# Latent gates in the last scan stage: sigmoid on ScalarE, or exponential on ScalarE and one-plus and reciprocal on VectorE

## The chip, the cores and the metric

The kernel runs on one core of a Trainium2 chip. The metric is the device time of one execution in microseconds (us), the median of several runs.

## The reference

Two layers of a hybrid sequence model, for 1024 prompt positions and 8 sample sequences of 16 new positions each, 1152 positions in all, everything in f32. Per layer:

```python
proj = h @ P['w_in'][l]
pr, zA, cq, ckv, kr, zB, sq, sk, sv, zC, gates = _split(proj, IN_SIZES)
yA, S1, shift1 = rwkv7_branch(pr, shift0, S0, P, l)       # a recurrence over time, 8 heads of 64
yB, ckv1, kr1 = mla_branch(cq, ckv, kr, ckv0, kr0, q_pos, k_pos, P, l)
yC, k1, v1 = sb_branch(sq, sk, sv, k0, v0, q_pos, k_pos)
merged = (gA * ((yA * jax.nn.silu(zA)) @ P['w_br_rwkv'][l])
          + gB * ((yB * jax.nn.silu(zB)) @ P['w_br_mla'][l])
          + gC * ((yC * jax.nn.silu(zC)) @ P['w_br_sb'][l]))
```

The change concerns `silu(zB)`, the gate of the latent attention branch: silu(z) = z times sigmoid(z) = z / (1 + exp(-z)). Half of its 512 columns (two pieces of 128 by 1152) are made in the stage that the change touches.

## The kernel before

A layer is a row of stages; between two stages all engines meet at a barrier. The recurrence (`rwkv`) takes two heads at a time, so there are four rounds `h` = 0 to 3. Each round has a stage `rwkv_solve` and then a stage `rwkv_fused(..., h, nx)`, which runs the scan of round `h` and, beside it, prepares round `nx` = `h + 1`. In the last round there is nothing to prepare (`nx` is None, `prep` is False). TensorE then fills its free time with the latent gates instead: `GATE_FILL`, six units of eight matmuls (one unit is z for 384 positions of one piece, `hT` times `w_piece`, L1052). This last stage occurs once in each layer, so twice in the kernel.

The scan goes over 16 chunks of 64 positions, one after another, and each needs the state of the one before. In chunk `n`:

- TensorE multiplies the state (L1101) and does one fill matmul ("mid").
- VectorE adds this to `z_solved` (L1282, semaphore `u_added`).
- TensorE makes the state's update from it (L1104) and the outputs (L1107), and does one fill matmul ("end").
- VectorE makes the new state (L1288, semaphore `s_scaled`), and TensorE's next chunk waits for it. A decayed copy of the state comes from GpSimd (L1015).

A program's fill matmul is two instructions in the trace, since f32 goes through TensorE in two passes. `gate_chunk` says in which chunk a unit's results are taken: units 0 and 1 ahead of chunk 0, units 2 to 5 in chunks 2, 6, 10 and 14. For a unit, ScalarE waits for the unit's last matmul and writes the sigmoid of the PSUM bank to `temp` (L1133). VectorE waits for that and multiplies it by the bank (`latent_gates`, L1273, semaphore `g_made`). VectorE does this in its own program order: behind the state of chunk 2, 6, 10 or 14 and ahead of the `z_solved` addition of the next chunk. Units from 2 on reuse one of two banks, so a unit's first matmul waits for the `g_made` of the unit two before it.

Beside this the engines normalise finished groups of outputs. VectorE forms sums (L1225 to L1229) at chunks 3, 7, 12 and behind the scan. ScalarE makes the reciprocal root as Ln and Exp (L1203, L1204) at `n` = 4, 8, 13 and 16. VectorE multiplies (L1234) at 5, 10, 14 and 16, TensorE transposes (L1067) ahead of chunks 11 and 15 and at the end, and VectorE applies the gate of this branch (L1239, L1240). ScalarE also copies two chunks' outputs behind each odd chunk (L1197, L1198).

ScalarE can only compute functions of the table set that it has loaded. The program loads a set by `preload_act_table_set`; where an activation needs a function that the active set lacks, the compiler puts a load ahead of it. `own(...)` makes an engine wait for its own instruction before it starts the next.

Of the kernel before, what the change touches and what calls it, by code (L numbers as in the profile page):

```python
# [8 lines left out]
ALU = mybir.AluOpType  # L9
ACT = mybir.ActivationFunctionType  # L10
# [15 lines left out]
NTG = T // TG  # L26
# [877 lines left out]
def rwkv_fused(nc, S, A, O, l, ps, con, hT, yg, zg, ahead, R, h, nx):  # L904
# [3 lines left out]
    V, ACTE = nc.vector, nc.scalar  # L908
# [4 lines left out]
             "state_out", "u_ready", "u_added", "y_ready", "y_copied", "s_ready", "s_scaled",  # L913
             "stat_in", "stat_out", "y_normed", "y_turned", "y_gated", "y_stored", "z_gated", "sd_made", "g_sigmoid", "g_made", "g_stored", "ahead_loaded", "ends_stored", "vec", "act_own")
    with S.stage(*names) as (block, sb, (w0_loaded, w1_loaded, par_done, fill_ready, free0, free1, summed, exps_done,
                                         z_sigmoid, shifted, squared, maxed, rooted, prod_done, r_done, k_stored, rv_stored,
                                         state_out, u_ready, u_added, y_ready, y_copied, s_ready, s_scaled,
                                         stat_in, stat_out, y_normed, y_turned, y_gated, y_stored, z_gated, sd_made, g_sigmoid, g_made, g_stored, ahead_loaded, ends_stored, vec, act_own)):
        free = (free0, free1)
# [32 lines left out]
        def cols(g):  # L952
            return slice(TG * g, TG * g + TG)
# [169 lines left out]
        def _(act):  # L1123
            own = InOrder(act, act_own)

            def evacuate(n):
# [5 lines left out]
                if kind == "g":  # L1132
                    ACTE.activation(t[g // NTG][:, c], src, ACT.Sigmoid).then_inc(g_sigmoid, 1)  # L1133
                    return
# [27 lines left out]
            if scan:  # L1162
                ACTE.activation(t[2][:, :], R.zs[h % 2][:, :], ACT.Sigmoid).then_inc(z_sigmoid, 1)
            for n in range(-1, NCK + 1):
                for q in range(len(fills)):
                    if chunk_of(q) == n:
                        evacuate(q)
                if n == 1:
                    ACTE.preload_act_table_set("natural_log_exp_and_others")
# [37 lines left out]
        def _(dve):  # L1207
# [60 lines left out]
            def latent_gates(n):  # L1268
                for q in range(len(fills)):
                    if not prep and chunk_of(q) == n:  # L1270
                        dve.wait_ge(g_sigmoid, q + 1)
                        c = cols(q % NTG)
                        V.tensor_tensor(t[q // NTG][:, c], t[q // NTG][:, c], ps[:, q % 2, 0:TG], ALU.mult).then_inc(g_made, 1)  # L1273

# [1562 lines left out]
```

## Time and profile before

| what | us |
|---|---|
| median of 3 runs | 4704.79 (4702.94 to 4711.39) |
| the profiled execution, its own time | 4707.36 |
| its span, first to last instruction | 4705.5 |
| last scan stage of layer 0, in the span | 712.5 to 793.6 |
| last scan stage of layer 1, in the span | 3057.4 to 3138.7 |

The profiled execution took 2.6 us more than the median of the runs. Times inside a stage are given from the span's start. A row of the timeline has the start, how long it took, the engine, the line, the operation and its tiles, how many instructions were merged in it, and in brackets the idle time of the engine ahead of it and what ended that.

### The profile page before, as it was taken

The page shows a single profiled execution, that of the slowest core. Times are in us where ns is not written, and L with a number is a line of the kernel's source. Part 1 is how long each engine was busy: PE and PEld are TensorE (multiplying, and loading weights), DVE is VectorE, ACT ScalarE, POOL GpSimd, SP SyncE. Part 2 cuts the span into 40 slices and gives each one's busy share as a digit, 9 for nine tenths or more (in the row PEclk, how much of TensorE's full clock was granted, in tenths as well). Part 3 has the DMA queues.
Part 4 walks back from the last instruction along what each step waited for, and adds up shares of the span by engine and source line. Part 5 has one row for each costly group of instructions (what it writes and reads, how often), then busy time and mean ns, then how long its engine had stood idle before and what let it go on. Part 6 is the DMA issues. An engine that isn't in the chain of part 4 may idle for free. (4 is left out here: it accounts for less than half of the span.)

```text
span 4705.5 us, 74875 instructions
## 1 busy us (share of the span) xinstructions
PE 4334.4 (92%) x29488; PEld 3017.3 (64%) x29488; DVE 2280.0 (48%) x4684; ACT 1643.2 (35%) x3886; POOL 814.2 (17%) x980
## 2 busy tenths in 40 slices
PE   7999998989989989999979999989888999899999
PEld 3666665667666667777436666655666566677774
DVE  2556664345524453534425665633455244535344
ACT  4333433445523442211043334333555234421220
POOL 0011010000010015544300110000000100245443
PEclk9999998999999999999989999999999999999999
DMA  5110012010021112222241210120100211123222
GB/s 195 23 35 13 28 25 87 14 36 14 12 87 56 53 65 92 95 102 76 85 192 23 35 15 26 25 88 17 31 16 11 87 58 57 70 88 111 89 72 84
DMA packets 150655, 280.77 MB, mean 60 GB/s; under 512 B 51546, under 2 KB 77402, under 8 KB 145059
## 3 DMA queue, kind: packets, MB, share of 16 engines
q1 hardware_dynamic: 150306, 275.99, 18.3%
q8 instruction: 236, 3.87, 0.4%
q14 instruction: 113, 0.92, 0.1%
HBM read 230.96 MB, written 42.62 MB: 58 GB/s over the span
## 5 line engine op out<-in xcount | busy, mean ns | idle before, releaser
L1054 PE MATMUL banks<-hT,w_piece 128*128 128x384 f32 x1536 | 545.2, 496 | 4.4 <-ACT raw L1159 4.1
L1054 PEld LDWEIGHTS banks<-hT,w_piece 128*128 128x128 f32 x1536 | 279.4, 193 | 171.6 <-issue 11.8
L2233 PE MATMUL banks<-hT,w_piece 128*128 128x384 f32 x1056 | 354.1, 489 | 1.5 <-ACT sb_gate_raw L2343 1.5
L2233 PEld LDWEIGHTS banks<-hT,w_piece 128*128 128x128 f32 x1056 | 196.1, 190 | 141.4 <-issue 16.6
L1999 DVE SCALAR_TENSOR_TENSOR keysT<-banks,gains,rstd 64x128 f32<-64x128 f32 (+1 forms) x272 | 112.1, 412 | 252.9 <-ACT rstd L1913 250.4
L2689 DVE TENSOR_TENSOR gate_quarters<-gate_kept,banks 128x288 f32<-128x288 f32 x144 | 65.4, 454 | 298.4 <-PE banks L2552 293.4
L2640 ACT ACTIVATE gate_kept<-banks 128x288 f32<-128x288 f32 x144 | 59.0, 410 | 431.9 <-PE banks L2552 431.9
L2689 DVE TENSOR_TENSOR branch_quarters<-branch_kept,banks 128x288 f32<-128x288 f32 x144 | 65.4, 454 | 265.0 <-PE banks L2552 264.7
L2405 DVE TENSOR_TENSOR_SCAN left<-pass,zero 128x384 f32<-128x384 f32 (+7 forms) x144 | 190.5, 1323 | 5.0
L2402 DVE TENSOR_TENSOR pass<-pass,constants 128x128 f32<-128x128 f32 x128 | 40.8, 319 | 312.8 <-ACT take L2354 310.2
L1015 POOL TENSOR_TENSOR state_decayed<-state,decay_of_chunk 128x128 f32<-128x128 f32 x120 | 85.9, 716 | 547.4 <-DVE state L1288 547.4
L1831 PE MATMUL banks<-keysT,queriesT 96*128 96x512 f32 (+3 forms) x384 | 155.3, 514 | 8.7 <-DVE queriesT L1999 8.7
L2552 PE MATMUL banks<-hT,w_gate_ahead 128*128 128x288 f32 x576 | 153.6, 418 | 7.7 <-PEq L132 7.4
L2552 PE MATMUL banks<-y_branch,w_branch 128*128 128x288 f32 x576 | 155.4, 406 | 0.0
L2552 PE MATMUL banks<-hT,w_gate 128*128 128x288 f32 x576 | 147.5, 406 | 0.0
L2552 PEld LDWEIGHTS banks<-hT,w_gate_ahead 128*128 128x128 f32 x576 | 112.7, 196 | 41.4 <-issue 9.3
L1929 ACT ACTIVATE exponentials<-banks,maximum 128x384 f32<-128x384 f32 (+4 forms) x144 | 104.1, 723 | 91.8 <-DVE maximum L2012 90.1
L1940 ACT ACTIVATE exponentialsT<-banks 128x512 f32<-128x512 f32 (+3 forms) x208 | 94.9, 488 | 115.8 <-PE banks L1843 114.9
L2213 POOL TENSOR_TENSOR sb_outT<-sb_outT,sb_gate 128x128 f32<-128x128 f32 x72 | 34.9, 484 | 579.3 <-ACT sb_outT L2375 578.2
L2230 PE MATMUL banks<-w_piece,hT 128*128 128x128 f32 x1152 | 132.7, 276 | 0.0
L2644 ACT ACTIVATE gate_quarters<-gate_quarters 128x288 f32<-128x288 f32 x144 | 63.5, 441 | 195.6 <-DVE gate_quarters L2689 195.1
L2230 PEld LDWEIGHTS banks<-w_piece,hT 128*128 128x128 f32 x1152 | 130.2, 192 | 1.0
(425 smaller groups left out, 9801.8 us busy)
## 6 DMA issues: line engine op xcount, KB each, us to landing
w_piece<-in_w_cols SPq DMA_DIRECT2D x66, 512.0 KB, 4.4
w_ada<-in_w_ada SPq DMA_DIRECT2D x24, 1024.0 KB, 9.6
w_gate_ahead<-in_w_cols SPq DMA_DIRECT2D x48, 512.0 KB, 4.3
w_branch<-in_w_br SPq DMA_DIRECT2D x96, 256.0 KB, 2.9
w_gate<-in_w_cols SPq DMA_DIRECT2D x48, 512.0 KB, 4.3
y_branch<-y_gated SPq DMA_DIRECT2D x12, 1152.0 KB, 8.0
sb_cached_keysT<-in_sbkT SPq DMA_DIRECT2D x8, 1024.0 KB, 7.6
sb_cached_values<-in_sbv SPq DMA_DIRECT2D x8, 1024.0 KB, 5.1
```

The lines of the kernel that those rows point to most:

```text
L1015: G.tensor_tensor(SD[:, :], ST[:, :], R.pend[h % 2][:, n + 1:n + 2].broadcast_to([P, P]), ALU.mult).then_inc(sd_made, 1)
L1054: last = mm(dst, w[0 if kind in ("k", "v") else 1][:, k, :], hT[:, k, c], start=(k == 0), stop=(k == KD - 1))
L1831: last = mm(ps[:, b0 + a // 512, 0:e - a], Q[hh][:, P * i:P * i + P], K[hh][:, a:e], start=True, stop=True)
L1929: do(E[u % 3][:, 0:width(u)], sbank(u)[:, 0:width(u)], ACT.Exp, bias=mx[:, u:u + 1], scale=scale, accum_out=rsum[:, u:u + 1]).then_inc(exp ...
L1940: do(ET[:, s % 4, units[u][3], 0:cnt, :].rearrange("p q n -> p (q n)"), ps[:, ring_bank(("t", u, g)), 0:P * cnt], Copy).then_inc(ring_free, 1)
L1999: ins = V.scalar_tensor_tensor(to[hh][0:64, c], ps[hc, bank[n], at], par[hc, gain:gain + 1], rs[x % 2][hc, at], ALU.mult, ALU.mult)
L2230: last = mm(ps[:, bank[n], P * q:P * q + P], hT[:, k, P * i:P * i + P], w_of[wn][:, k, :], start=(k == 0), stop=(k == KD - 1))
L2233: last = mm(ps[:, bank[n], 0:TG], w_of[wn][:, k, :], hT[:, k, TG * g:TG * g + TG], start=(k == 0), stop=(k == KD - 1))
L2405: own(V.tensor_tensor_scan(mine[:, 0:n][:, ::-1], G[k][:, 0:n][:, ::-1], zero[:, 0:1].broadcast_to([P, n]), 1.0, ALU.mult, ALU.add))
L2552: ins = mm(ps[:, bank, 0:TQ], w[:, k, :], b[:, k, :], start=(first and k == 0), stop=(k == half - 1), skip_group_check=True)
L2644: do(gq[:, q, :], gq[:, q, :], ACT.Tanh, scale=0.5).then_inc(tanh_done, 1)
L2689: own(V.tensor_tensor(dst, src, ps[:, bank, 0:TQ], ALU.add), added)
```

## The change

In the last stage, ScalarE writes exp(-z) instead of sigmoid(z), and VectorE adds one and takes the reciprocal before it multiplies by z. The set with both the logarithm and the exponential is loaded right behind the one sigmoid that stays (that of the recurrence's own gate), ahead of all six units, instead of at `n` = 1. The other `rwkv_fused` stages keep their instructions.

```diff
@@ scalar, evacuate
                 act.wait_ge(fill_ready, n + 1)
                 if kind == "g":
-                    ACTE.activation(t[g // NTG][:, c], src, ACT.Sigmoid).then_inc(g_sigmoid, 1)
+                    ACTE.activation(t[g // NTG][:, c], src, ACT.Exp, scale=-1.0).then_inc(g_exp, 1)
                     return
@@ scalar
             if scan:
                 ACTE.activation(t[2][:, :], R.zs[h % 2][:, :], ACT.Sigmoid).then_inc(z_sigmoid, 1)
+            if not prep:
+                ACTE.preload_act_table_set("natural_log_exp_and_others")
             for n in range(-1, NCK + 1):
...
-                if n == 1:
+                if prep and n == 1:
                     ACTE.preload_act_table_set("natural_log_exp_and_others")
@@ vector, latent_gates
-                        dve.wait_ge(g_sigmoid, q + 1)
+                        dve.wait_ge(g_exp, q + 1)
                         c = cols(q % NTG)
+                        own(V.tensor_scalar(t[q // NTG][:, c], t[q // NTG][:, c], 1.0, None, ALU.add))
+                        own(V.reciprocal(t[q // NTG][:, c], t[q // NTG][:, c]))
                         V.tensor_tensor(t[q // NTG][:, c], t[q // NTG][:, c], ps[:, q % 2, 0:TG], ALU.mult).then_inc(g_made, 1)
```

ScalarE's instructions from the start of layer 1's last stage to chunk 4, before (`temp_25` holds the gates, `silu_z_16` the recurrence's gate):

```order
L1161 ACT_TABLE_LOAD
L1163 ACTIVATE temp_25<-silu_z_16 128x1152
L1133 ACTIVATE temp_25<-banks 128x384 x2
L1169 ACT_TABLE_LOAD
L1197 ACTIVATE z_solved<-banks 64x128
L1198 ACTIVATE z_solved<-banks 64x128
L1133 ACT_TABLE_LOAD
L1133 ACTIVATE temp_25<-banks 128x384
L1197 ACTIVATE z_solved<-banks 64x128
L1198 ACTIVATE z_solved<-banks 64x128
L1203 ACT_TABLE_LOAD
L1203 ACTIVATE statistics<-statistics,constants 128x2
```

And now, at the same place, up to the Exp of the first statistics:

```order
L1161 ACT_TABLE_LOAD
L1163 ACTIVATE temp_25<-silu_z_16 128x1152
L1165 ACT_TABLE_LOAD
L1133 ACTIVATE temp_25<-banks 128x384 x2
L1199 ACTIVATE z_solved<-banks 64x128
L1200 ACTIVATE z_solved<-banks 64x128
L1133 ACTIVATE temp_25<-banks 128x384
L1199 ACTIVATE z_solved<-banks 64x128
L1200 ACTIVATE z_solved<-banks 64x128
L1205 ACTIVATE statistics<-statistics,constants 128x2
L1206 ACTIVATE statistics<-statistics 128x2
```

The load of L1169 moved ahead of the first two units, and no other load is left in the stage: ScalarE has 3298 instructions where it had 3322 (runs of equal ones counted once), 12 fewer in each of the two stages.

VectorE's instructions around the first two units and chunk 0 of the same stage, before:

```order
L1266 TENSOR_TENSOR sample_states<-banks,decay_of_chunk_16 128x512
L1273 TENSOR_TENSOR temp_25<-temp_25,banks 128x384 x2
L1282 TENSOR_TENSOR bk_and_vu_rows<-z_solved,banks 64x128
L1288 SCALAR_TENSOR_TENSOR state<-banks,decay_of_chunk_16,state_decayed 64x64 x2
L1282 TENSOR_TENSOR bk_and_vu_rows<-z_solved,banks 64x128
```

And now:

```order
L1268 TENSOR_TENSOR sample_states<-banks,decay_of_chunk_16 128x512
L1275 TENSOR_SCALAR temp_25<-temp_25 128x384
L1276 RECIPROCAL temp_25<-temp_25 128x384
L1277 TENSOR_TENSOR temp_25<-temp_25,banks 128x384
L1275 TENSOR_SCALAR temp_25<-temp_25 128x384
L1276 RECIPROCAL temp_25<-temp_25 128x384
L1277 TENSOR_TENSOR temp_25<-temp_25,banks 128x384
L1286 TENSOR_TENSOR bk_and_vu_rows<-z_solved,banks 64x128
L1292 SCALAR_TENSOR_TENSOR state<-banks,decay_of_chunk_16,state_decayed 64x64 x2
```

Four instructions came in ahead of the first addition to `z_solved`.

VectorE's instructions at chunk 14, the last unit, before:

```order
L1288 SCALAR_TENSOR_TENSOR state<-banks,decay_of_chunk_16,state_decayed 64x64 x2
L1273 TENSOR_TENSOR temp_25<-temp_25,banks 128x384
L1234 TENSOR_TENSOR z_solved<-z_solved,statistics 128x384
L1282 TENSOR_TENSOR bk_and_vu_rows<-z_solved,banks 64x128
L1288 SCALAR_TENSOR_TENSOR state<-banks,decay_of_chunk_16,state_decayed 64x64 x2
```

And now:

```order
L1292 SCALAR_TENSOR_TENSOR state<-banks,decay_of_chunk_16,state_decayed 64x64 x2
L1275 TENSOR_SCALAR temp_25<-temp_25 128x384
L1276 RECIPROCAL temp_25<-temp_25 128x384
L1277 TENSOR_TENSOR temp_25<-temp_25,banks 128x384
L1236 TENSOR_TENSOR z_solved<-z_solved,statistics 128x384
L1286 TENSOR_TENSOR bk_and_vu_rows<-z_solved,banks 64x128
```

The two new instructions stand between the state of chunk 14 and both things that TensorE needs next, the normalised outputs and the addition of chunk 15.

## Rows read from the trace of the kernel before

**Rows 1.** The page: busy time of each engine.

```profile
PE 4334.4 (92%) x29488; PEld 3017.3 (64%) x29488; DVE 2280.0 (48%) x4684; ACT 1643.2 (35%) x3886; POOL 814.2 (17%) x980
```

**Rows 2.** Both last scan stages: busy PE, PEld, DVE, ACT, POOL; clock; DMA, GB/s.

```profile
712.50:793.60 81.10, 60.17 (x261) 37.07 (x261) 41.73 (x103) 28.42 (x45) 8.71 (x16) 0.88 0.10 34
3057.40:3138.70 81.30, 58.53 (x261) 36.04 (x262) 41.72 (x103) 28.42 (x45) 8.71 (x16) 0.90 0.10 34
```

**Rows 3.** Timeline of VectorE, layer 0, first two units to chunk 3.

```profile
731.34 1.02 DVE L1273 TENSOR_TENSOR temp<-temp,banks 128x384 f32<-128x384 f32 x2
733.77 0.29 DVE L1282 TENSOR_TENSOR bk_and_vu_rows<-z_solved,banks 64x128 f32<-64x128 f32 x1 [1.41 <-PE banks L1101]
...
736.03 0.28 DVE L1282 TENSOR_TENSOR bk_and_vu_rows<-z_solved,banks 64x128 f32<-64x128 f32 x1 [0.73 <-PE banks L1101]
...
738.27 0.29 DVE L1282 TENSOR_TENSOR bk_and_vu_rows<-z_solved,banks 64x128 f32<-64x128 f32 x1 [0.75 <-PE banks L1101]
...
740.83 0.55 DVE L1273 TENSOR_TENSOR temp<-temp,banks 128x384 f32<-128x384 f32 x1 [1.05 <-ACT temp L1133]
741.30 0.27 DVE L1282 TENSOR_TENSOR bk_and_vu_rows<-z_solved,banks 64x128 f32<-64x128 f32 x1
```

**Rows 4.** Timeline of TensorE at the same places.

```profile
731.95 1.56 PE L1052 MATMUL banks<-hT,w_piece 128*128 128x384 f32 x4 [1.45 <-DVE temp L1273]
...
739.34 0.86 PE L1052 MATMUL banks<-hT,w_piece 128*128 128x384 f32 x2
...
741.63 0.49 PE L1104 MATMUL banks<-bk_and_vu_rows 128*128 128x128 f32 x2 [0.56 <-DVE bk_and_vu_rows L1282]
```

**Rows 5.** ScalarE, layer 0: timeline of chunk 2; the gates' activations of the whole stage.

```profile
737.85 1.28 ACT L1133 ACT_TABLE_LOAD   x1
740.24 0.49 ACT L1133 ACTIVATE temp<-banks 128x384 f32<-128x384 f32 x1 [1.10 <-PE banks L1052]
...
L1133 ACT ACTIVATE temp<-banks 128x384 f32<-128x384 f32 x6 | 2.9, 490 | 15.5 <-PE banks L1052 15.5
```

**Rows 6.** VectorE's reciprocal and scalar operation of this shape, both in other stages, whole kernel.

```profile
L1572 DVE RECIPROCAL rope_rstd<-rope_rstd 128x384 f32<-128x384 f32 x12 | 30.6, 2553 | 19.7 <-ACT rope_rstd L1533 19.6
L2019 DVE TENSOR_SCALAR exponentials<-exponentials,row_sums 128x384 f32<-128x384 f32 x32 | 13.4, 420 | 1.2
```

**Rows 7.** Timeline of layer 1 at chunk 14: TensorE, ScalarE, VectorE.

```profile
3121.14 0.86 PE L1052 MATMUL banks<-hT,w_piece 128*128 128x384 f32 x2
...
3122.79 1.28 ACT L1133 ACT_TABLE_LOAD   x1
3124.08 0.49 ACT L1133 ACTIVATE temp<-banks 128x384 f32<-128x384 f32 x1
...
3125.75 0.90 PE L1067 MATMUL banks<-constants,z_solved 128*128 128x128 f32 x3 [3.75 <-DVE z_solved L1234]
```

**Rows 8.** The same of layer 0: TensorE's last fill, and ScalarE's activation.

```profile
777.71 0.86 PE L1052 MATMUL banks<-hT,w_piece 128*128 128x384 f32 x2
...
779.05 0.49 ACT L1133 ACTIVATE temp<-banks 128x384 f32<-128x384 f32 x1
```

**Rows 9.** Timeline of layer 0 behind the scan: ScalarE, VectorE.

```profile
787.05 1.28 ACT L1204 ACT_TABLE_LOAD   x1
...
787.39 0.62 DVE L1240 SCALAR_TENSOR_TENSOR k_shifted<-k_shifted,parameters,silu_z 128x384 f32<-128x384 f32 x1
788.65 0.42 DVE L1234 TENSOR_TENSOR z_solved<-z_solved,statistics 128x256 f32<-128x256 f32 x1 [0.64 <-ACT statistics L1204]
```

**Rows 10.** Granted clock around the idle time of TensorE, both layers.

```profile
772.00:776.00 4.00, 2.86 (x11) 2.16 (x12) 1.70 (x6) 1.90 (x4) 0.40 (x1) 0.75 0.00 0
3126.00:3130.00 4.00, 2.62 (x11) 2.14 (x10) 1.09 (x4) 0.87 (x3) 0.00 (x0) 0.50 0.37 147
```

**Rows 11.** TensorE in layer 0 at the lower clock: two chunks' L1104.

```profile
773.14 0.49 PE L1104 MATMUL banks<-bk_and_vu_rows 128*128 128x128 f32 x2 [1.65 <-DVE bk_and_vu_rows L1282]
...
776.84 0.63 PE L1104 MATMUL banks<-bk_and_vu_rows 128*128 128x128 f32 x2
```

More of the change, by code:

```diff
@@ L913, in rwkv_fused @@
              "state_out", "u_ready", "u_added", "y_ready", "y_copied", "s_ready", "s_scaled",
-             "stat_in", "stat_out", "y_normed", "y_turned", "y_gated", "y_stored", "z_gated", "sd_made", "g_sigmoid", "g_made", "g_stored", "ahead_loaded", "ends_stored", "vec", "act_own")
+             "stat_in", "stat_out", "y_normed", "y_turned", "y_gated", "y_stored", "z_gated", "sd_made", "g_exp", "g_made", "g_stored", "ahead_loaded", "ends_stored", "vec", "act_own")
     with S.stage(*names) as (block, sb, (w0_loaded, w1_loaded, par_done, fill_ready, free0, free1, summed, exps_done,
@@ L917, in rwkv_fused @@
                                          state_out, u_ready, u_added, y_ready, y_copied, s_ready, s_scaled,
-                                         stat_in, stat_out, y_normed, y_turned, y_gated, y_stored, z_gated, sd_made, g_sigmoid, g_made, g_stored, ahead_loaded, ends_stored, vec, act_own)):
+                                         stat_in, stat_out, y_normed, y_turned, y_gated, y_stored, z_gated, sd_made, g_exp, g_made, g_stored, ahead_loaded, ends_stored, vec, act_own)):
         free = (free0, free1)
```

## The prediction

> **What bounds the kernel now.** I read the page first: TensorE is busy for 92% of the span, VectorE for 48%, ScalarE for 35% [rows 1]. That is an average over the whole kernel, and the change touches two stages of some 81 us each, 162 of 4705.5 us. So I read those two by themselves. In them TensorE is busy for 60.2 and 58.5 us of 81, VectorE for 41.7 and ScalarE for 28.4 [rows 2]. None of the three is full. A stage like this is bound by a chain from engine to engine, and the timeline shows which links it has.
>
> An ordinary chunk of the scan takes 736.03 to 738.27, 2.24 us from one addition L1282 to the next, and VectorE waits 0.73 to 0.75 us ahead of each for TensorE [rows 3]. That is the slack that VectorE has in a chunk without other work. At chunk 2 it is different. VectorE waits 1.05 us for ScalarE, then multiplies the unit, and the addition of chunk 3 starts only behind that, at 741.30. TensorE waits 0.56 us for this addition [rows 3, 4]. So where a unit is taken, VectorE's own program order puts the gate on the path of the recurrence, with no slack left. This happens at chunks 2, 6, 10 and 14. The first two units are taken ahead of chunk 0: TensorE waits 1.45 us for the first of them (it needs the bank), and then VectorE waits 1.41 us for TensorE [rows 3, 4].
>
> Next I ask what ScalarE is late for. At chunk 2 its table load starts at 737.85 and is over at 739.13. Then it still waits 1.10 us for TensorE, whose last fill matmul ends at 739.34 + 0.86 = 740.20, and the activation starts at 740.24 [rows 4, 5]. So the load is hidden there. Over the stage of layer 0, ScalarE's idle time ahead of these activations is 15.5 us, all of it ended by TensorE's fill [rows 5]; chunks 6 and 10 have the same 1.1 us in the timeline. Only chunk 14 differs. In layer 1 the last fill ends at 3121.14 + 0.86 = 3122.00, but a row of three loads ends at 3124.08 [rows 7].
>
> **What the change removes.** Twelve table loads in each stage, 24 x 1.283 = 30.8 us of ScalarE's time. What of it lies on the path is little:
> - Chunks 2, 6 and 10, both layers: nothing, since TensorE's fill ends last.
> - Chunk 14, layer 1: the activation could start at 3122.00 + 0.04 = 3122.04 in place of 3124.08, a gain of 2.04 [rows 7].
> - Chunk 14, layer 0: at 777.71 + 0.86 + 0.04 = 778.61 in place of 779.05, a gain of 0.44 [rows 8].
> - Behind the scan: VectorE waits 0.64 us for the statistics, which stand behind one load. VectorE starts 788.65 - 787.05 - 1.28 = 0.32 us behind the load's end, so without the load it could start at 787.37. It is itself busy until 787.39 + 0.62 = 788.01, so it starts at about 788.04 in place of 788.65 [rows 9]. A gain of 0.61, in both layers, 1.22.
>
> Together 2.04 + 0.44 + 1.22 = 3.7 us. The load that moves ahead of the units costs nothing: of the 15.5 us of idle time, some 12 lie ahead of these two.
>
> The Trainium skill ("ScalarE: Activation LUTs", section "What ACT_TABLE_LOAD costs") gives 2.66 us for a switch of sets, of which 1.38 us are a drain. Here an activation starts within 0.02 us of a load's end (3122.79 + 1.28 against 3124.08), so by the rows a switch costs 1.28 us; by the page the 24 would hold 64 us of ScalarE.
>
> **What the change adds.** Per unit, VectorE gets an addition and a reciprocal of 128 x 384 in SBUF. The trace has both shapes elsewhere. The reciprocal took 2.553 us in each of 12, and the operation with a scalar 0.420 us [rows 6]. With some 0.03 us between instructions that wait for each other, a unit gets 0.45 + 2.58 = 3.03 us more. The scalar operation of the row takes its factor from a column and this one a constant, which may differ by a tenth of a microsecond either way; the reciprocal has the same shape, type and place, so I hold it for certain within 0.1.
>
> - Units 2 to 5: ScalarE's result comes when it came before (exponential and sigmoid are both one activation). VectorE then starts its addition to `z_solved` 3.03 us later, and TensorE, which had waited already, waits 3.03 us more. 4 x 3.03 = 12.1 us per layer. Nothing can be caught up later, since the chunks run one after another at 2.24 us, and TensorE's own work in one fills nearly all of this.
> - Units 0 and 1, ahead of chunk 0: VectorE needs 6.06 us more, and 1.41 us of that is the wait that it has now ahead of the first addition [rows 3]. TensorE is released by the first unit, after 3.03, and is then ready well ahead of VectorE. 6.06 - 1.41 = 4.65 us per layer.
>
> That makes 16.8 us per layer, 33.5 in all, less 3.7 is 29.8 us. What waits behind VectorE in those 3 us is the whole scan: TensorE's update, ScalarE's copies, GpSimd's decayed state. The statistics for chunks 11 and 15 stand behind the gates on VectorE too and move along with them, at no extra price.
>
> **The clock.** TensorE's idle stretches grow from 0.56 to about 3.6 us at chunks 2 and 6, from 1.45 to 4.5 ahead of chunk 0, and by as much at chunk 10, where TensorE waits for the normalised outputs that stand behind the unit on VectorE. In the trace an idle stretch of 3.75 us [rows 7] is followed by the lower level, 1.2 in place of 2.4 GHz (0.50 in the rows behind it), and after some shorter ones in layer 0 the clock fell too, for part of a stretch (0.75) [rows 10]. A chunk in layer 0 at the lower level took 773.14 to 776.84, 3.70 us, so 1.46 more than the ordinary 2.24 [rows 11]. So each of the four longer stalls ahead of chunk 14 probably brings a low stretch of about this kind. Its price is between nothing (it falls within the stall, or beside VectorE's sums, where TensorE waits anyway) and about 2.9 us (two chunks). I take 0.9 each, near the lower end: the stalls at chunks 2 and 6 are followed by a chunk in which VectorE's sums make TensorE wait already (as the 1.65 us ahead of 773.14 [rows 11]), and the stretch begins within the stall. 8 x 0.9 = 7.2 us. The stall at chunk 14 is followed by the low level already now.
>
> Sum: 29.8 + 7.2 = 37.0 us. Against the profiled execution that is 4707.4 + 37 = 4744; against the median of the runs, which is 2.6 us lower, 4704.8 + 37 = 4742 us.
>
> **The rivals.** A measurement of this kernel can tell about 0.2%, 9.4 us, from no change.
> - The clock stays at its upper level. For it: the 1.45 us ahead of chunk 0 left no slow chunk behind them [rows 3, 4]. Against it: 3.75 us did [rows 7, 10]. It gives 29.8, so 4735 us, within the range.
> - The clock stays low through the scans. All 16 chunks of both layers at 3.70 instead of 2.24 would be 32 x 1.46 = 47 us more, 4782 us. Against it: in layer 0 the level was back within one chunk or two.
> - VectorE's work is hidden, and ScalarE decides. If what ends VectorE's waits of 1.05 us were the loads, and the new operations fitted in its idle time (39.4 of 81 us per stage; both stages together get 36 us), the kernel would be faster: the 1.28 us of a load at each of eight units and twice at the end, 12.8 us, so 4692 us. It decides only if VectorE could run the gates in another order than ahead of the next addition, which an engine with one instruction stream can't. The Trainium skill's rule to group activations by their table set ("ScalarE: Activation LUTs", section "Rules for kernel authors") speaks for this way, and the row at chunk 2 against it, where TensorE's fill ends last.
> - The reciprocal is as fast as other operations of its width, 0.56 us: a unit gets 1.04 us more, the first two 0.67 together, so 4.8 us per layer, 9.7 less 3.7 is 6 us, no change that can be told, 4711 us. The twelve equal rows speak against it.
>
> **How the numbers follow.** I give the forecast with some price of the clock, 25 to 50 us slower, 0.83; the upper rival (over 53 us) 0.07; something that hides most of the added work, within 9.4 us, 0.04; faster 0.02; and 0.04 for a slowdown of 10 to 25 us through slack that I overlooked. Slower by over 0.2% is then 0.94, the same 0.04, faster 0.02. For the range I take 29.8 less 5 us for slack in the first units and the small terms, and 29.8 plus the full 8 x 2.9 = 23 us of clock: 4730 to 4758 us. The likeliest value lies below the middle, because I hold the full price for rare.
>
> **What would show it.** In the changed kernel's trace: no load of tables in the two stages but two at the start; a reciprocal of 2.55 us x12 at the line of the gates; an addition of 0.4 us; TensorE waits of about 3.6 us for the addition to `z_solved` at chunks 2 and 6; 4.5 us ahead of chunk 0; both stages about 98 to 102 us long in place of 81; granted clock below the 0.88 and 0.90 of now; nothing else in the kernel changed by more than 1 us. I would be wrong in the main thing if the stages grew by less than 10 us each, which would mean slack between VectorE and TensorE that the rows don't show, and wrong in the clock if single chunks of 3.7 us were absent or were most of the scan.

## The result, and the profile after

The changed kernel took 4734.54 us (median of 5 runs, 4722.78 to 4738.90) against 4706.47 us (5 runs, 4702.94 to 4712.83) on the same chip: ratio 1.0054, interval 1.0039 to 1.0069. By the ratio it is 25 us slower, by the medians 28. A second set of runs gave 1.0046 (1.0030 to 1.0062), 22 us. The forecast was 37. The profiled execution took 4722.78 us, the shortest of its five; its span is 4720.9 us, 15.4 above that of before (4705.5).

The page, busy time of each engine (for [rows 1]), and below it the windows of the two last scan stages (for [rows 2]: length, busy PE, PEld, DVE, ACT, POOL, granted clock, DMA share, GB/s):

```profile
PE 4331.1 (92%) x29488; PEld 3016.0 (64%) x29488; DVE 2312.9 (49%) x4708; ACT 1617.3 (34%) x3862; POOL 814.0 (17%) x980
```

```profile
705.90:806.20 100.30, 68.07 (x261) 42.92 (x262) 59.21 (x115) 13.03 (x33) 8.73 (x16) 0.80 0.08 28
3065.70:3165.00 99.30, 67.12 (x262) 42.49 (x262) 59.19 (x115) 13.02 (x33) 8.73 (x16) 0.79 0.08 28
```

The stages grew by 19.2 and 18.0 us to 100.3 and 99.3 (98 to 102 was forecast), 37.2 together, and VectorE's busy time in each by 17.5. ScalarE has twelve instructions fewer in each. The groups of VectorE at the gates, layer 0 (six units):

```profile
L1276 DVE RECIPROCAL temp<-temp 128x384 f32<-128x384 f32 x6 | 15.3, 2553 | 0.2
L1277 DVE TENSOR_TENSOR temp<-temp,banks 128x384 f32<-128x384 f32 x6 | 3.3, 554 | 0.2
L1275 DVE TENSOR_SCALAR temp<-temp 128x384 f32<-128x384 f32 x6 | 2.2, 359 | 4.2 <-ACT temp L1133 4.2
```

And the timelines of VectorE, TensorE and ScalarE at the places of [rows 3 to 5]: first two units, chunk 2, and the later stalls.

```profile
724.65 0.36 DVE L1275 TENSOR_SCALAR temp<-temp 128x384 f32<-128x384 f32 x1
...
731.67 0.29 DVE L1286 TENSOR_TENSOR bk_and_vu_rows<-z_solved,banks 64x128 f32<-64x128 f32 x1
...
740.16 0.36 DVE L1275 TENSOR_SCALAR temp<-temp 128x384 f32<-128x384 f32 x1 [1.05 <-ACT temp L1133]
740.55 2.55 DVE L1276 RECIPROCAL temp<-temp 128x384 f32<-128x384 f32 x1
743.14 0.55 DVE L1277 TENSOR_TENSOR temp<-temp,banks 128x384 f32<-128x384 f32 x1
743.61 0.27 DVE L1286 TENSOR_TENSOR bk_and_vu_rows<-z_solved,banks 64x128 f32<-64x128 f32 x1
```

```profile
728.24 2.93 PE L1052 MATMUL banks<-hT,w_piece 128*128 128x384 f32 x4 [4.43 <-DVE temp L1277]
...
743.94 0.49 PE L1104 MATMUL banks<-bk_and_vu_rows 128*128 128x128 f32 x2 [3.54 <-DVE bk_and_vu_rows L1286]
744.66 1.53 PE L1052 MATMUL banks<-hT,w_piece 128*128 128x384 f32 x2
...
774.85 1.12 PE L1067 MATMUL banks<-constants,z_solved 128*128 128x128 f32 x4 [4.69 <-DVE z_solved L1236]
793.88 0.90 PE L1067 MATMUL banks<-constants,z_solved 128*128 128x128 f32 x3 [4.69 <-DVE z_solved L1236]
```

```profile
708.33 1.28 ACT L1165 ACT_TABLE_LOAD   x1
...
739.56 0.49 ACT L1133 ACTIVATE temp<-banks 128x384 f32<-128x384 f32 x1 [2.40 <-PE banks L1052]
```

Chunk 2 reads as before, with one thing put in. VectorE waits the same 1.05 us for ScalarE; ScalarE, with no load any more, waits 2.40 us for TensorE where it had a load of 1.28 and a wait of 1.10. So the load was hidden, to within 0.02 us. Then come 0.36 + 2.55 us of new work, and TensorE waits 3.54 us where it waited 0.56. Behind that stall the same two fill matmuls take 1.53 us where they took 0.86 [rows 4]: the clock fell to its lower level (granted 0.65 from 746 to 749 us, and 1.00 in the 3 us behind that).

Since the chunks run in a fixed chain, the time from one addition to `z_solved` to the next gives the whole stage by chunk. These are differences of the starts in VectorE's timeline, in us (chunk 1 is the time from chunk 0's addition to chunk 1's; L0, L1 are the layers):

| chunk | 1 | 2 | 3 | 4 | 5 | 6 | 7 | 8 | 9 | 10 | 11 | 12 | 13 | 14 | 15 | sum |
|---|---|---|---|---|---|---|---|---|---|---|---|---|---|---|---|---|
| before, L0 | 2.26 | 2.24 | 3.03 | 3.02 | 2.26 | 2.25 | 3.03 | 4.09 | 2.26 | 2.24 | 4.63 | 3.61 | 4.11 | 3.07 | 6.26 | 48.36 |
| after, L0 | 3.68 | 2.25 | 6.01 | 3.12 | 3.33 | 2.25 | 6.01 | 4.39 | 3.28 | 2.24 | 8.28 | 4.39 | 4.11 | 2.24 | 8.06 | 63.64 |
| before, L1 | 2.26 | 2.25 | 3.03 | 3.02 | 2.26 | 2.25 | 3.03 | 4.09 | 2.26 | 2.24 | 4.63 | 3.61 | 4.11 | 2.25 | 7.11 | 48.40 |
| after, L1 | 3.09 | 2.25 | 6.01 | 3.69 | 2.40 | 2.24 | 6.02 | 4.40 | 3.13 | 2.25 | 8.63 | 4.03 | 4.10 | 2.25 | 8.06 | 62.55 |

Chunks 3 and 7 are 2.98 us longer: the new work and nothing else. Chunks 1, 5 and 9, which stand behind the stalls, are 1.42, 1.07 and 1.02 longer in layer 0, and 0.83, 0.14 and 0.87 in layer 1: the clock. Where the low stretch lies differently, chunk 4 has a part of it (3.69 for 3.02 in layer 1).

So the stages grew by what was forecast, to the microsecond, and yet the kernel is 22 to 28 us slower and not 37. The difference lies in a stage that the change doesn't touch. Windows of the latent pairs stage (no line of it differs), both layers, before and after:

```profile
945.30:1330.70 385.40, 335.51 (x2521) 254.97 (x2521) 203.84 (x571) 206.58 (x518) 26.49 (x103) 0.94 0.07 20
3290.50:3675.60 385.10, 335.31 (x2521) 254.73 (x2521) 203.75 (x570) 206.43 (x518) 26.36 (x103) 0.94 0.07 20
```

```profile
957.60:1335.00 377.40, 327.12 (x2521) 249.10 (x2521) 203.83 (x570) 206.92 (x518) 26.57 (x103) 0.97 0.07 21
3314.90:3692.30 377.40, 327.70 (x2521) 250.32 (x2521) 203.74 (x570) 206.91 (x518) 26.48 (x103) 0.97 0.07 21
```

The instructions are the same in number, VectorE and ScalarE are busy for as long as before, but TensorE is granted 0.97 in place of 0.94, and is busy for 8 us less. It starts with the first matmuls, before and after in layer 0:

```profile
945.31 3.75 PE L1780 MATMUL banks<-latentT,weights_ahead 128*128 128x256 f32 x8 [3.22 <-PEq L132]
```

```profile
957.63 1.97 PE L1784 MATMUL banks<-latentT,weights_ahead 128*128 128x256 f32 x8 [3.21 <-PEq L132]
```

TensorE idles for 3.2 us as it enters this stage. Before, the first eight matmuls then run at the lower level (3.75 us), after at the upper (1.97). In layer 1 the first eight are slow in both kernels, but in the changed one the next sixteen are at full speed already. Before and after:

```profile
3290.45 3.75 PE L1780 MATMUL banks<-latentT,weights_ahead 128*128 128x256 f32 x8 [3.40 <-PEq L132]
3293.99 3.11 PE L1799 MATMUL banks<-weights_ahead,latentT 128*128 128x128 f32 x16
```

```profile
3314.86 3.65 PE L1784 MATMUL banks<-latentT,weights_ahead 128*128 128x256 f32 x8 [3.21 <-PEq L132]
3318.33 1.97 PE L1803 MATMUL banks<-weights_ahead,latentT 128*128 128x128 f32 x16
```

The granted clock of the first 6 us of the stage in layer 0, before and after:

```profile
945.30:951.30 6.00, 5.99 (x20) 5.28 (x21) 0.56 (x2) 2.02 (x3) 0.53 (x2) 0.50 0.78 165
```

```profile
957.60:963.60 6.00, 5.97 (x36) 5.51 (x37) 0.56 (x2) 3.03 (x5) 0.55 (x2) 1.00 0.79 171
```

The difference goes on behind the entry. In pieces of 64 us, the second is at 0.97 before and 1.00 after:

```profile
1009.30:1073.30 64.00, 59.83 (x467) 46.07 (x467) 36.05 (x96) 38.31 (x91) 4.70 (x21) 0.97 0.02 6
```

```profile
1021.60:1085.60 64.00, 59.22 (x481) 46.45 (x480) 37.01 (x98) 39.32 (x95) 5.17 (x22) 1.00 0.02 7
```

The sum over the profiled executions: +37.2 in the last scan stages, -15.7 in the two latent pairs stages, 21.5 together. The spans differ by 15.4. The remaining -6.1 is a sum of moves in both directions in stages that the change doesn't touch: -7.5 in the first preparing scan stage of layer 0 (87.1 us before, 79.6 after), +4.3 in a later one of that layer (105.3 and 109.6), +3.3 in the first of layer 1 (80.4 and 83.7), and smaller ones that sum to -6.2.

### The profile page after: what moved, and what is told of

It is laid out like the page before. It is cut to its first block and busy times, and to the rows that moved or that the text cites. A ratio compares the mean times of both kernels' runs of the same rounds, so it can differ in the third digit from the quotient of the medians.

```text
span 4720.9 us, 74875 instructions
## 1 busy us (share of the span) xinstructions
PE 4331.1 (92%) x29488; PEld 3016.0 (64%) x29488; DVE 2312.9 (49%) x4708; ACT 1617.3 (34%) x3862; POOL 814.0 (17%) x980
```

## The experiments

In all, "stages" are the two last scan stages, "pairs" the two latent pairs stages; what they gained or lost is against 81.1 + 81.3 and 385.4 + 385.1 of before. Lengths of stages are read to 0.1 us, so a sum of four holds to about 0.2.

**Each kernel once more.** The first question was whether 385 and 377 belong to the kernels or to single executions.

> The kernel before once more, for a second profile of it. If lengths outside the change move by coincidence of the clock, some of its stages differ from those of its first profile by 2 to 8 us, the latent pairs stages (385.4 and 385.2 us before) among them, with a sum within 8 us. If a kernel's stages repeat, all of them are within 1 us, and the 8 us at latent pairs belong to the change. The two last scan stages are 81 us in any case.

> The changed kernel once more, for a second profile. Two questions are open after the first: its two last scan stages grew by 19.3 and 18.3 us, 37.6 together, but its span only by 15.4, since the stages outside the change were shorter by 22 us in that one execution. If those 22 us are a coincidence of TensorE's clock in this one execution, the two stages are again 99 to 101 us long here, the other stages differ from the kernel before by less than 12 us in sum, and the span is 4726 to 4738. If the change itself shortens what follows (the latent pairs stage was 8 us shorter in both layers), that stage is again shorter by 8 us twice.

The kernel before: stages 81.1 and 81.1, pairs 385.4 and 385.1, as in its first profile (its runs: ratio 0.9988, 0.9976 to 1.0001). The changed kernel: stages 99.2 and 99.3, pairs 378.9 and 377.0. One window of each, layer 0:

```profile
943.40:1328.80 385.40, 335.46 (x2521) 254.92 (x2521) 203.79 (x571) 206.86 (x518) 26.55 (x103) 0.94 0.07 20
```

```profile
956.20:1335.10 378.90, 328.72 (x2520) 250.31 (x2521) 203.78 (x570) 206.54 (x518) 26.55 (x103) 0.96 0.07 21
```

So in the four pairs stages of each kernel's two profiles, the two kernels don't overlap. The first preparing stage took 86.3 and 82.3 us in these profiles, and 80 to 87 in others.

**The exponential without VectorE's part.** The changed kernel; it leaves out the addition of one and the reciprocal, so that the gates hold z times exp(-z). It shows what the loads were worth.

```
-                        own(V.tensor_scalar(t[q // NTG][:, c], t[q // NTG][:, c], 1.0, None, ALU.add))
-                        own(V.reciprocal(t[q // NTG][:, c], t[q // NTG][:, c]))
```

> The changed kernel without VectorE's two new operations: ScalarE writes exp(-z), the table loads are gone, and VectorE multiplies as before; left out is adding one and the reciprocal, so half of the latent gates are z times exp(-z). Theory one, that VectorE's new work is the price and the loads were mostly hidden: against before 3.7 us less, more exactly 0.5 + 0.6 in layer 0 and 2.0 + 0.6 in layer 1, and up to 2 more where TensorE's clock stays up; the stages take 78 to 80.5 us each. Theory two, that the loads were on the path: 12.8 us less at least, up to 30.8 (all 24 loads of 1.283 us), the stages 66 to 75 us each.

Ratio 0.9952 (0.9937 to 0.9966). The windows of both stages:

```profile
705.00:784.60 79.60, 59.75 (x262) 36.63 (x262) 41.73 (x103) 13.02 (x33) 8.73 (x16) 0.89 0.10 35
3046.50:3126.10 79.60, 59.75 (x261) 36.62 (x261) 41.71 (x103) 13.06 (x33) 8.75 (x16) 0.89 0.10 35
```

They are 1.5 and 1.7 us shorter: 24 loads, 30.8 us of ScalarE, were worth 3.2 us. Chunks 1 to 13 are the same as before within 0.02 us each; only the steps to chunks 14 and 15 changed (5.43 for 6.26 in layer 0; in layer 1 5.42 for 7.11, but 3.03 for 2.25 ahead of it, where the lower clock now fell). The sum of the two steps is 0.9 us less in each layer. The kernel as a whole gained 23 us, seven times as much, and 15.5 of that is pairs at 377.5 us in both layers. That the loads were "worth 0.5%" would be the wrong reading of the time alone: in the stages they were worth 3.2 us.

**VectorE's part without the exponential.** The kernel before, with an addition of one and a reciprocal on a spare tile ahead of each multiplication; sigmoid and loads stay.

```
+            spare = None if prep else sb("spare_gate", [P, TG])
...
+                        own(V.tensor_scalar(spare[:, :], t[q // NTG][:, c], 1.0, None, ALU.add))
+                        own(V.reciprocal(spare[:, :], spare[:, :]))
```

> The kernel before, with its sigmoid and all its table loads, and an addition and a reciprocal of 128 x 384 on VectorE ahead of each multiplication, into a spare tile that nothing reads. Theory one: each of units 2 to 5 costs 2.97 us, the first two 4.6 together, so 16.5 us per layer and some 4 more for TensorE's lower clock: stages of 101 to 103 us, 41 us more than before over both, slightly above the changed kernel, by the 3.7 us of the loads. Theory two, that the loads decide and VectorE's work fits beside them: the stages stay within 3 us of before.

Ratio 1.0077 (1.0061 to 1.0094), stages 101.8 and 102.0:

```profile
709.50:811.30 101.80, 66.82 (x261) 42.15 (x261) 59.22 (x115) 28.41 (x45) 8.74 (x16) 0.80 0.08 27
```

That is +41.4 us, and with the loads' 3.2 taken off it is within 1 us of the change's 37.2: the two parts add up. Here pairs took 379.7 and 384.6, so only 6.2 us came back, and the kernel is 36 us slower. The less the pairs give back, the more of the stages' cost arrives in the time.

**A wait and nothing else.** If pairs depend only on the moment at which TensorE gets there, a useless wait must move them as well. The kernel before, with two reciprocals on a spare tile (filled with ones at the start of the stage) behind the scan, ahead of the gate of the last quarter.

```
             if scan:
+                if not prep:
+                    own(V.reciprocal(spare[:, 0:384], spare[:, 0:384]))
+                if not prep:
+                    own(V.reciprocal(spare[:, 0:128], spare[:, 0:128]))
                 gate(3, 4)
```

> The kernel before, with nothing of the change, and two reciprocals (384 and 128 columns of a spare tile) on VectorE ahead of the last gate of the last scan stage, in both layers: a pure wait of 3.5 us, of which 0.85 lie beside a wait for TensorE, so each of these stages gets 2.6 us longer. Question: why the latent pairs stage took 385 us in both profiles of before and 377 to 379 in both of the changed kernel and of the one with the exponential alone. [...] The wait then brings the latent pairs stages to 377 to 379 us in both layers, and the kernel is faster in spite of it: 2 x 2.6 us more, 2 x 7.8 less, so 8 to 12 us less than before. Theory B: the change itself, its tables or its instructions, shortens that stage; or nothing does and it was chance. Then the latent pairs stages stay at 385 us and the kernel is 5 us slower.

The stages took 83.8 us each, 2.7 and 2.5 longer. Pairs, both layers:

```profile
947.80:1324.90 377.10, 327.40 (x2521) 250.45 (x2521) 203.82 (x571) 206.35 (x518) 26.50 (x103) 0.97 0.07 21
3293.00:3669.80 376.80, 327.21 (x2521) 250.32 (x2521) 203.81 (x570) 206.19 (x518) 26.44 (x103) 0.97 0.07 21
```

8.3 us shorter in both layers, with no load gone and no new work at the gates. The time as a whole: 0.9993 (0.9980 to 1.0006), no change that can be told, though the two parts sum to -11.4. In the profiled execution the stages that nothing touches took 7.0 us more, and its span is 4.4 us below that of before. A shorter wait, one reciprocal of 320 columns in that place (`spare[:, 0:320]`), which took 2.15 us:

> As wait_long, with one reciprocal of 320 columns in place of two: 2.2 us of work, 1.3 us of wait in each of the two stages. If it is the moment at which the stages behind it meet TensorE's clock that decides, the latent pairs stage begins here with about the same relation to the clock as in the two profiles of the changed kernel, and takes 377 to 379 us in both layers. If wait_long was an accident, it takes 385 us as in both profiles of before.

Stages 82.4 and 84.1, so 1.3 and 2.8 us longer. The wait accounts for 1.3 of each; in layer 1, some 1.6 us more lie at chunks 9 and 10, ahead of the new reciprocal, where the clock fell (granted 0.61 from 3104 to 3107 us; steps of 2.89 and 3.22 us for 2.26 and 2.24). Pairs again at 0.97 and 0.96:

```profile
947.30:1324.60 377.30, 327.66 (x2521) 250.34 (x2521) 203.73 (x570) 206.50 (x518) 26.50 (x103) 0.97 0.07 21
3296.20:3674.40 378.20, 328.29 (x2520) 249.97 (x2521) 203.75 (x570) 206.55 (x518) 26.55 (x103) 0.96 0.07 21
```

Ratio 0.9976 (0.9965 to 0.9988). A kernel that only does useless work is 11 us faster. That its pairs are the reason isn't shown: the profiled execution took 4706.23 us, the second longest of its twelve (median 4693.32), and its span is only 1.1 us below that of before, since the untouched stages took 9.8 us more in it. What is on record of all twelve is the granted clock over the whole span, 0.972 in the median, against 0.968 for the 29 executions of before at its side. So the gain goes with a higher clock, in stages that only a profile of one of the faster executions could name. The longer wait's median is 0.969, against 0.967.

**The stalls filled with matmuls.** The changed kernel, with matmuls into a bank that nothing reads, in the stalls ahead of chunk 0 and at chunks 3, 7, 10 and 14. It separates the clock from VectorE's work.

```
+            def idle_work(count):
+                if not prep:
+                    for _ in range(count):
+                        mm(ps[:, 7, 0:TG], con("blockones"), hT[:, 0, 0:TG], start=True, stop=True)
...
+            idle_work(6)
             fill(behind)
...
                 fill(mid)
+                idle_work(5 if n in (3, 7) else 0)
...
                 if n == 10:
+                    idle_work(6)
                     pe.wait_ge(y_normed, 2)
...
                 if n == 14:
+                    pe.wait_ge(y_gated, 2)
+                    idle_work(6)
                     pe.wait_ge(y_normed, 3)
-                    pe.wait_ge(y_gated, 2)
```

> The changed kernel, with matmuls whose results nobody reads on TensorE in the five stalls of each of the two stages: 6 ahead of the first fill of unit 2, 5 ahead of the updates of chunks 3 and 7, 6 ahead of each of the transposes behind chunks 10 and 14, into a bank that is free then, some 0.7 us each at the upper clock. If the lower clock behind the stalls costs the stages something, they get shorter: by the trace of the changed kernel chunks at the lower level are 1.4 us longer, and what is left of the growth of 19.3 and 18.3 us, after 16.4 for VectorE and less 1.0 and 2.6 for the loads, is 3.9 and 4.5 us. So 96 us each in place of 100.3 and 99.3, with a granted clock of 0.95 and more in their first 85 us. If the clock costs nothing, the stages stay within 1 us. The whole kernel may differ by up to 16 us from this through the latent pairs stages.

```profile
712.50:806.60 94.10, 76.06 (x317) 45.54 (x318) 59.18 (x115) 13.02 (x33) 8.72 (x16) 0.94 0.08 30
3065.90:3158.40 92.50, 74.50 (x318) 45.06 (x318) 59.18 (x115) 12.98 (x33) 8.72 (x16) 0.95 0.09 30
```

The stages are 6.2 and 6.8 us shorter than those of the changed kernel, with 56 matmul instructions (28 matmuls of the program) more in each. By the same measure of chunks, layer 1 now has 2.25, 2.25, 6.01, 3.03, 2.26, 2.24, 6.02, 4.09, 2.25: chunks 1, 5 and 9 are back to their old length, and the two chunks with units are not. The rows at chunk 2 of layer 0 show it as well:

```profile
749.12 0.49 PE L1111 MATMUL banks<-bk_and_vu_rows 128*128 128x128 f32 x2 [0.32 <-DVE bk_and_vu_rows L1295]
749.84 0.86 PE L1052 MATMUL banks<-hT,w_piece 128*128 128x384 f32 x2
```

The fill pair takes 0.86 us again. Part of the gain lies where the kernel before was slow too (the step to chunk 15, 7.50 for 8.06, and the end), so the 13.0 us are probably more than what the change itself cost in clock. What the added matmuls themselves cost isn't separated. Ratio 1.0042 (1.0025 to 1.0059), which can't be told from the changed kernel's 1.0054 and 1.0046.

**The gate taken where VectorE has slack.** If the path is VectorE's order at chunks 2, 6, 10 and 14, the multiplication may be put later, where its operand is long there and VectorE has its 0.7 us of idle time anyway. On the kernel before:

```
-                    if not prep and chunk_of(q) == n:
+                    if not prep and (-1, -1, 4, 8, 13, 15)[q] == n:
```

> The kernel before (sigmoid and table loads as they were), with VectorE's multiplications of units 2 to 5 moved in its order from chunks 2, 6, 10 and 14 to chunks 4, 8, 13 and 15, where ScalarE's result has long been there and VectorE waits 0.75 us for TensorE anyway. If VectorE's order at those places is what binds the scan, the stalls of 0.56 us at chunks 2 and 6 go, and those at chunk 10 and 14 shrink by VectorE's wait and the multiplication: 0.76 + 0.76 + 1.5 + 2.0 (layer 0) or 3.5 (layer 1), so stages of 74 to 76.5 us in place of 81. If only the sum of VectorE's work counts, or ScalarE's loads, nothing changes. The kernel: 10 to 12 us less in the stages, and 16 more or nothing in the latent pairs stages.

```profile
740.38 0.56 DVE L1273 TENSOR_TENSOR temp<-temp,banks 128x384 f32<-128x384 f32 x1
741.03 0.28 DVE L1282 TENSOR_TENSOR bk_and_vu_rows<-z_solved,banks 64x128 f32<-64x128 f32 x1
```

The multiplication now has no idle time ahead of it, and the addition behind it starts 2.19 us behind the one before (738.84). The stages took 74.5 and 73.1 us, 14.8 shorter together. The time: 0.9979 (0.9967 to 0.9992), 10 us. The profiled execution was 17.7 us shorter, so on this kernel too the medians don't give what the stages do.

The same edit on the changed kernel:

> The changed kernel, with VectorE's addition, reciprocal and multiplication of units 2 to 5 moved together to chunks 4, 8, 13 and 15. They don't wait for ScalarE there, but the block of 0.39 + 2.58 + 0.55 = 3.5 us still stands as one piece in VectorE's order. If it is the block's length against the slack of 0.75 us in a chunk that counts, each costs 2.8 us, where the changed kernel's cost 3.73 (0.76 + 2.97) at chunks 2 and 6 and 4.5 and more at 10 and 14: stages about 5 to 7 us shorter than the changed kernel's 100 and 99, and 19 us longer than in mult_later and three_acts_later, whose only difference it is. If waiting for ScalarE had been the price, they would be as short as in mult_later, 74 us.

Stages 90.4 and 90.5, 9 to 10 us shorter than those of the changed kernel (5 to 7 were expected), but 16 to 17 longer than with the sigmoid in the same order. The slack of 0.7 us holds the multiplication and not 3 us of new work. Ratio 1.0026 (1.0014 to 1.0038).

**The gate made on ScalarE alone.** ScalarE has the idle time and VectorE not. Exp, Ln and Exp are in one set of tables: exp(-ln(1 + exp(-z))) is the sigmoid.

```
-                    ACTE.activation(t[g // NTG][:, c], src, ACT.Exp, scale=-1.0).then_inc(g_exp, 1)
+                    own(ACTE.activation(t[g // NTG][:, c], src, ACT.Exp, scale=-1.0))
+                    own(ACTE.activation(t[g // NTG][:, c], t[g // NTG][:, c], ACT.Ln, bias=con("eps")[:, 3:4]))
+                    ACTE.activation(t[g // NTG][:, c], t[g // NTG][:, c], ACT.Exp, scale=-1.0).then_inc(g_exp, 1)
```

VectorE only multiplies (the fourth column of the constant `eps` is 1 here). In the order of before:

> The three activations (exp, ln with one added, exp) and VectorE's multiplication alone, at their old places, chunks 2, 6, 10 and 14. VectorE waits there for ScalarE, and two more activations lie between the fill and the multiplication: 2 x 0.5 us and their own waits. Units 2 to 5 cost 1.1 us each more than in the run exp_alone, whose stages are 0.7 us shorter than before's: so 3.5 to 4.5 us longer than before in each stage, 85 us, a third of what the reciprocals on VectorE cost. Against three_acts_later it shows what the place of the multiplication is worth: 10 to 12 us per stage.

```profile
736.26 0.55 DVE L1277 TENSOR_TENSOR temp<-temp,banks 128x384 f32<-128x384 f32 x1 [2.25 <-ACT temp L1135]
```

VectorE waits 2.25 us for ScalarE where it waited 1.05: the two more activations stand on the path instead. Stages 85.2 and 85.1; 1.0002 (0.9992 to 1.0013). And with the multiplications later as well:

> A third way to the same gates: ScalarE takes exp(-z), then ln(1 + that), then exp(-that), all of one table set, so no loads and no reciprocal on VectorE, which only multiplies, and that at chunks 4, 8, 13 and 15 as in the run mult_later. ScalarE gets 1.0 us more per unit, where it has 40 us of idle time. If VectorE's order alone binds, the stages are as short as in mult_later, 74 to 76 us, less 0.6 us for the load behind the scan. If the table loads had been a cost of their own, it is shorter than mult_later by 3 us and more per stage.

```profile
735.10 0.49 ACT L1133 ACTIVATE temp<-banks 128x384 f32<-128x384 f32 x1 [2.40 <-PE banks L1052]
735.62 0.61 ACT L1134 ACTIVATE temp<-temp,constants 128x384 f32<-128x384 f32 x1
736.27 0.52 ACT L1135 ACTIVATE temp<-temp 128x384 f32<-128x384 f32 x1
```

Stages 72.7 and 73.9, pairs 375.9 and 377.3, ratio 0.9940 (0.9924 to 0.9955): 28 us faster than before, and the fastest kernel of this study. Most of that isn't the gate without a sigmoid table. Against the kernel with the sigmoid and the multiplication later, the stages are 1.0 us shorter together (1.8 in layer 0, and 0.8 longer in layer 1). Of the other 17 us between the two kernels' times, 9.2 are pairs, so clock, and the rest isn't placed. In the stages the later multiplication is worth 14.8 us of the 15.8. What the three activations show is that the idea of the change, no sigmoid table in this stage, costs nothing once the gate's work is off VectorE and off the path.

All kernels together, in us against before; the last column is the ratio less one, by the median of before:

| kernel | stages | pairs | the two | measured |
|---|---|---|---|---|
| before, again | -0.2 | 0.0 | -0.2 | -6 |
| changed | +37.2 | -15.7 | +21.5 | +25 |
| changed, again | +36.1 | -14.6 | +21.5 | +22 |
| exponential alone | -3.2 | -15.5 | -18.7 | -23 |
| VectorE's part alone | +41.4 | -6.2 | +35.2 | +36 |
| longer wait | +5.2 | -16.6 | -11.4 | -3 |
| shorter wait | +4.1 | -15.0 | -10.9 | -11 |
| stalls filled | +24.2 | -14.0 | +10.2 | +20 |
| multiplication later | -14.8 | -8.1 | -22.9 | -10 |
| changed, later | +18.5 | -14.8 | +3.7 | +12 |
| three activations | +7.9 | -4.2 | +3.7 | +1 |
| three, later | -15.8 | -17.3 | -33.1 | -28 |

The two parts, from one profiled execution each, give the measured time within 6 us in eight of the twelve, and are 8 to 13 us too low in the other four. That is partly luck: in the profiled executions themselves, the stages outside the two parts took between 6.1 us less and 9.8 us more than in the first profile of before. So the two parts are most of it and not all.

## Why the prediction was right, and where it was wrong

**What bounds the stage: right.** A chain over VectorE's program order, with the table loads hidden behind TensorE's fill. The rival in which the loads decide (4692 us) is out: without the 24 loads and without new work, the stages gained 3.2 us, and chunks 1 to 13 nothing. The Trainium skill ("ScalarE: Activation LUTs", section "What ACT_TABLE_LOAD costs") gives 2.66 us for a switch of sets; an estimate by it is 64 us of ScalarE for the 24. Its number for the load itself, 1283 ns, agrees with the rows here. Its drain of 1.38 us doesn't show on either side of a load: at the start of the changed stage in layer 0, an activation starts 0.02 us behind one load's end (707.15 against 705.85 + 1.28), and the next load 0.02 us behind the activation's (708.33 against 707.15 + 1.16).

**VectorE's additional work: right.** The forecast had 3.03 us per unit; measured 2.98 at chunks 3 and 7. The reciprocal is the 2.553 us of [rows 6], so the rival with a cheap reciprocal is out. The scalar operation took 0.36 and not 0.42. The first two units moved the start of chunk 0 by 4.59 us relative to the first gate (724.65 to 731.67 against 731.34 to 733.77), forecast 4.65. Stalls: 3.54 at chunks 2 and 6 (3.6 said), 4.43 ahead of chunk 0 (4.5), 4.69 at chunk 10.

**What the loads gave back: right in size, not in its parts.** 3.2 us against 3.7, by the run without VectorE's part. At chunk 14 of layer 1 it was 1.69 less 0.78, so 0.9, in place of 2.04, because a stretch at the lower clock moved in ahead of it; in layer 0 it was 0.9 in place of 0.44.

**The clock: right in size, shown in part.** Forecast 8 x 0.9 = 7.2 us. Of the 37.2 us, VectorE's work is (4 x 2.98 + 4.50) + (4 x 2.98 + 4.41) = 32.8 (the starts of chunk 0 by the stages' starts), and the loads gave back 3.2; this leaves 7.6. The stalls filled with matmuls show that there is a price of the clock and that it lies behind the stalls; they don't give its size, since their 13 us hold more than the change's own. The rival with the clock low all through (4782) is out, that with the clock untouched (4735) too: it would give stages of 81.2 + 14.9 = 96.1, which were 99.3 and 100.3. The measured 4734.54 us is that rival's number all the same, so only the stages tell the two apart. That the forecast for the stages came out within 0.2 us is luck in part: its three terms are off by -0.7, +0.5 and +0.4 us, and the 0.9 per stall was picked from a range of 0 to 2.9.

**"Nothing else in the kernel changed by more than 1 us": wrong.** This is the step that failed. Both latent pairs stages became 8 us shorter, 15.7 in all, since TensorE's clock was 0.97 in them in place of 0.94. So the forecast of 4742 us, right about the stages, was 7.5 us too high for the median of the first runs and 11 for the second. As differences, 37 us stand against 25 to 28 and 22, so 9 to 15 too many. The second lies below the 25 to 50 us that the forecast held for likeliest. That it is no work saved there is shown: equal counts, equal busy time of VectorE and ScalarE, and the same 8 us in a kernel that only had a wait added. An added wait changes the program too; that it is the clock and not the place of the instructions rests on the granted clock of all profiles, below. The Trainium skill ("TensorE: Matmul & The Clock Gate", Part 1) says of the slow matmuls at a kernel's start that their number varies from run to run, and that their price is under 1% of a typical span. What shows here inside the kernel is of that size: 15.7 of 4705 us are 0.33%. But that is nearly half of the 37.2 us by which the change made its own stages longer, and within one kernel it came out the same in two profiles (385.4 and 385.1, both times).

What decides between 385 and 377 us can be read from the granted clock in the thirteen profiles, 26 pairs stages in all. The length goes with the time at the lower level (1.2 GHz): seven stages of 384.6 to 385.4 us were there for 43 to 44 us, three of 379.4 to 381.6 for 28 to 35, and sixteen of 375.8 to 378.9 for 19 to 27. And it goes with the entry. TensorE idles for 3.2 to 3.4 us ahead of the stage, and the clock falls about then. In nine stages it had fallen 0.65 to 1.34 us before the stage's first matmul, and then stayed low for the first 5.5 to 6.2 us; all seven long ones are among these, and the other two took 379.4 and 379.6. In the other seventeen it fell at most 0.60 us before the first matmul, or up to 0.24 behind it, and was up again sooner, or it didn't fall at all; none took more than 381.6. So a shift of the arrival by less than a microsecond is enough. No run was made to test this rule on an arrival chosen for it.

The other untouched stages that vary do so with the clock as well: the later scan stage that took 109.6 us in place of 105.3 was at the lower level for 14 us in place of 3. For the first preparing stage this is true only in part: it was there for 19 us where it took 87.1, but for 10 both where it took 79.6 and where it took 82.3.

Open: why the clock falls where it does, what else moves the first preparing stage, and whether the executions that weren't profiled had the pairs of the profiled one. With the stalls filled, the two parts and the span of the profiled execution agree (+10.2 and +10.6), and the measured time is +20, so there the other executions differ from the profiled one. Each run has only its mean granted clock on record, from 0.961 to 0.975, and can't say in which stage it was low.

## What to carry to other kernels

Before work is moved from an engine's table loads to another engine, look at what ended the wait of the activation behind the load: here TensorE did, and 30.8 us of loads were worth 3.2, while six reciprocals per stage in VectorE's order cost nearly their full length in the recurrence (33 of 35 us in VectorE's busy time). Put the work on the engine that has idle time (here ScalarE, three activations from one set) and take its result where the waiting engine has slack. Here the second alone was worth 14.8 us in the two stages, and the first alone made them 7.9 longer; the two together gave 15.8. And judge a change under half a per cent by stages and granted clock as well as by the whole time, since a stage that it doesn't touch can give or take 8 us.

## What the runs showed of the hardware that was not expected

A useless 2.15 us of VectorE behind each of two scans made the kernel 0.24% faster (0.9965 to 0.9988), with a granted clock of 0.972 in the median of its executions, against 0.968. In its profile the stages lost 4.1 us, and two stages 150 us further on gained 15.0, by a granted clock of 0.97 and 0.96 in place of 0.94; stages elsewhere lost 9.8. Table loads taken out moved the same two stages by 15.5 us. All seven of these stages, of 26, that took about 385 us had been entered with a clock that fell 0.65 us or more ahead of their first matmul. Filling TensorE's stalls of 3.5 to 4.7 us with matmuls into an unread bank gave 6.2 and 6.8 us per stage back, but nothing that could be told in the kernel's time.
